# A hybrid decoder step on one core: the first weight loaded in two parts by rows, conditioning blocks moved ahead, the first block issued from GpSimd

## What is computed

```python
mod = (jax.nn.silu(c) @ w_ada + b_ada)[:, None, :]          # w_ada: 1024 x 6144 per layer
sh1, sc1, g1, sh2, sc2, g2 = jnp.split(mod, 6, axis=-1)
hn = rmsnorm(x, norm1_g) * (1.0 + sc1) + sh1
proj = hn @ w_in                                            # w_in: 1024 x 2560 per layer
xl, gl, bs, cs, hs = jnp.split(proj, 5, axis=-1)
# ... convolutions, a recurrence, an output projection and a residual,
# then a second norm, a convolutional FFN (1024 -> 2 x 2816 -> 1024), a residual;
# after two layers a last norm
```

## Time and profile before

| | us |
|---|---|
| median of three runs | 1335.13 |
| the three runs | 1335.13, 1333.09, 1335.45 |
| the profiled execution's own time | 1333.17 |
| its span, first to last instruction | 1331.5 |
| PE busy in the span | 1309.1 (98%) |
| DVE, ACT, POOL busy | 712.3, 488.1, 47.6 |
| mean granted TensorE clock | 0.997 of full speed |

### The profile page before, as it was taken

How to read it: one execution, slowest core, us unless ns; L and a number is a source line. 1 busy time by engine, 2 the same in 40 slices (tenths; PEclk the granted TensorE clock), 3 DMA queues, 4 the chain that set the end, 5 groups by cost and what they waited for, 6 DMA issues and landing times.

```text
span 1331.5 us, 23749 instructions
## 1 busy us (share of the span) xinstructions
PE 1309.1 (98%) x9767; PEld 1249.5 (94%) x9767; DVE 712.3 (53%) x1260; ACT 488.1 (37%) x646; POOL 47.6 (4%) x94
## 2 busy tenths in 40 slices
PE   7999999999999999999999999999999999999998
PEld 6887888899999999999999888999999999999997
DVE  5555854775445443454587177377544454354445
ACT  5424752453223222232353376245323322123231
POOL 0300000000000000000110000000000000000001
PEclk9999999999999999999999999999999999999999
DMA  9654656422221221212233465312222222222202
GB/s 307 213 184 161 218 196 216 159 95 71 88 95 63 95 96 63 95 63 95 80 128 117 168 222 186 131 64 72 72 97 93 80 95 68 90 80 78 95 32 97
DMA packets 115837, 157.10 MB, mean 118 GB/s; under 512 B 3543, under 2 KB 108984, under 8 KB 110645
## 3 DMA queue, kind: packets, MB, share of 16 engines
q1 hardware_dynamic: 108413, 112.55, 25.7%
q0 software_dynamic: 7168, 43.47, 9.5%
q10 hardware_dynamic: 184, 0.06, 0.0%
HBM read 153.08 MB, written 2.99 MB: 117 GB/s over the span
## 4 chain that ended last, share of the span: by engine, by line
PE 90%; DVE 3%; DMA 3%; SPq 2%; ACT 1%; issue 1%; DVEq 0%; POOLq 0%; ACTq 0%
PE ps L385 25%; PE ps L387 24%; PE ps L386 24%; PE ps L404 4%; PE ps L406 3%; PE ps L405 3%; PE ps L451 3%; DMA ada_w<-in_w_ada 2%; DVE w_lo L1051 1%; DMA ada_first<-in_w_ada 1%; SPq L280 1%; PE ps L651 1%; SPq L271 1%; SPq L253 1%; ACT w_hi L746 0%
## 5 line engine op out<-in xcount | busy, mean ns | idle before, releaser
L385 PE MATMUL ps<-norm_hi,w_hi 128*128 128x288 f32 x1792 | 533.1, 297 | 0.0
L386 PE MATMUL ps<-norm_lo,w_hi 128*128 128x288 f32 x1792 | 528.6, 295 | 0.0
L387 PE MATMUL ps<-norm_hi,w_lo 128*128 128x288 f32 x1792 | 526.8, 294 | 0.0
L385 PEld LDWEIGHTS ps<-norm_hi,w_hi 128*128 128x128 f32 x1792 | 335.8, 187 | 16.8 <-issue 15.9
L387 PEld LDWEIGHTS ps<-norm_hi,w_lo 128*128 128x128 f32 x1792 | 337.4, 188 | 0.0
L386 PEld LDWEIGHTS ps<-norm_lo,w_hi 128*128 128x128 f32 x1792 | 336.4, 188 | 0.0
L1051 DVE TENSOR_TENSOR w_lo<-w_raw,w_hi 128x2048 fp32r<-128x2048 f32 x91 | 208.4, 2290 | 86.6 <-ACT w_hi L746 86.5
L746 ACT ACTIVATE w_hi<-w_raw 128x2048 fp32r<-128x2048 f32 x91 | 173.9, 1911 | 156.3 <-PE ps L387 152.0
L385 PE MATMUL ps<-mid_hi,w_hi 128*128 128x288 f32 x704 | 209.3, 297 | 0.0
L386 PE MATMUL ps<-mid_lo,w_hi 128*128 128x288 f32 x704 | 207.7, 295 | 0.0
L387 PE MATMUL ps<-mid_hi,w_lo 128*128 128x288 f32 x704 | 207.0, 294 | 0.0
(11 more groups left out here) (213 smaller groups left out, 1381.0 us busy)
## 6 DMA issues: line engine op xcount, KB each, us to landing
w_raw<-in_ffn_w_up SPq DMA_DIRECT2D x44, 1024.0 KB, 5.0
ada_w<-in_w_ada POOLq DMA_DIRECT2D x40, 1024.0 KB, 5.1
w_raw<-in_w_in SPq DMA_DIRECT2D x20, 1024.0 KB, 5.1
w_raw<-in_ffn_w_down SPq DMA_DIRECT2D x16, 1024.0 KB, 5.2
ada_first<-in_w_ada SPq DMA_DIRECT2D x8, 1024.0 KB, 10.4
w_raw<-in_w_out SPq DMA_DIRECT2D x8, 1024.0 KB, 5.4
w_raw<-in_ffn_w_down SPq DMA_DIRECT2D x8, 768.0 KB, 4.4
work<-in_x_prompt SPq DMA_DIRECT2D x4, 512.0 KB, 5.3
```

The source lines that it names most:

```text
L385: T.matmul(out, WH[:, r, k, c:c + P], xh[:, k, h, :], start=start, stop=False)
L386: T.matmul(out, WH[:, r, k, c:c + P], xl[:, k, h, :], start=False, stop=False)
L387: last = T.matmul(out, WL[:, r, k, c:c + P], xh[:, k, h, :], start=False, stop=stop)
```

## The change

Five things are changed, all in the first 60 us:

1. **Two parts by rows.** The first two pieces of `w_in` are no longer loaded whole. A load brings the row blocks 0 to 3 of a piece (512 KB, semaphore `raw_rows`), a later one the row blocks 4 to 7 (512 KB, `raw_full`). ACT's `head_split` waits for the part that it reads.
2. **Order of SP's queue.** Now: c, x, first rows of both pieces, block 1, block 2, later rows of both pieces, block 3, vectors and states. Block 2 still waits for product 0, block 3 for product 1.
3. **Block 0 from GpSimd.** Its two loads are issued by GpSimd, after its small constants and ahead of the zeroing of `gate_w`.
4. **Sigmoid table.** ACT's table for the sigmoid is loaded as its first instruction, ahead of the nine vector loads.
5. **The later rows' split moves.** ACT splits the later rows after `first_row(2)` instead of before `first_row(1)`, DVE's two `head_low` for them stand in the rounds 4 and 5, and PE waits for the slot that a tile needs (`lo_done` 3 for tiles 0 and 1, 4 for tile 2).

The core of the diff:

```diff
-            first_block(0)
-            for s in range(2):
-                load(s, s, a["w_in"][0:1, :, 256 * s:256 * s + 256])
+            def load_rows(part, s):
+
+                src = a["w_in"][0, :, 256 * s:256 * s + 256].rearrange("(k p) c -> p k c", p=P)
+                k = slice(0, KX // 2) if part == 0 else slice(KX // 2, KX)
+                sp.dma_start(RAW[:, s, k, :], src[:, k, :]).then_inc(raw_full[s] if part else raw_rows[s], 16)
+
+            load_rows(0, 0)
+            load_rows(0, 1)
             first_block(1)
+            first_block(2)
+            load_rows(1, 0)
+            load_rows(1, 1)
+            first_block(3)
             vectors(sp, 0, slice(NFIRST, None), v_in[0])
-            first_block(2)
-            first_block(3)
...
             nc.gpsimd.memset(EPST[:], EPS).then_inc(ident_ready, 1)
+            ada0 = a["w_ada"][0].rearrange("(k p) c -> p k c", p=P)
+            for j in range(2):
+                pool.dma_start(FIRST[0][:, :, j, :], ada0[:, :, j * D:j * D + 256]).then_inc(first_full[0], 16)
             nc.gpsimd.memset(BLK[:], 0.0).then_inc(pool_step, 1)
...
-                if k == KX // 2:
-                    pe.wait_ge(lo_done, 4)
                 for h in range(2):
                     if k % 2 == 0:
                         pe.wait_ge(norm_ready, k + h + 1)
                     for i in range(3):
+                        if k == KX // 2 and h == 0 and i != 1:
+                            pe.wait_ge(lo_done, 3 + i // 2)
...
             act.sem_inc(ada_rows_ready, 1)
+            act.preload_act_table(ACT.Sigmoid)
             vectors(act, 0, slice(0, NFIRST), v_first)
...
-                if part == 0:
-                    act.wait_ge(raw_full[s], 16)
+                act.wait_ge((raw_full if part else raw_rows)[s], 16)
...
-            head_split(0, 1)
-            head_split(1, 1)
             for b in range(1, 4):
                 first_row(b)
+                if b == 2:
+                    head_split(0, 1)
+                    head_split(1, 1)
...
-            head_low(0, 1)
-            head_low(1, 1)
             for b in range(1, 4):
                 first_modulation(b)
                 sample_part(1, MOD_SH1, 2 * b)
+                if b == 2:
+                    head_low(0, 1)
                 scaled(1, 2 * b + 1, rs0)
                 sample_part(1, MOD_SH1, 2 * b + 1)
                 norm_low(1, 2 * b)
+                if b == 2:
+                    head_low(1, 1)
```

More of the change, by code:

```diff
@@ L199, in hybrid_trunk_kernel @@
         raw_full = [sem("raw_full0"), sem("raw_full1")]
+        raw_rows = [sem("raw_rows0"), sem("raw_rows1")]
         hi_done, lo_done = sem("hi_done"), sem("lo_done")
```

## The result

The changed kernel is slower: 1338.51 us median of 8 runs (1337.17 to 1340.09), against 1334.62 (1333.09 to 1336.64) of 8 runs of the kernel before, ratio 1.0026 with a 95% interval of 1.0017 to 1.0035. The forecast was 1333.5 with a range of 1330.2 to 1336.9: wrong in sign, and outside its range.

What follows compares the result with a forecast made beforehand. Bound by transferred bytes until 38 us, then TensorE; product 3's start was followed: 46.04 - (43.1 + 2.2) = 0.7 us gained, taken from the runs' mean: 1334.2 - 0.7 = 1333.5, range 1330.2 to 1336.9.

Steps and rivals of the forecast that it cites:

- Bytes in front of the blocks: Loads ahead of conditioning blocks: block 1 3.0 us earlier, block 2 3.9, block 3 at 42.9, capping the gain at 3.1.
- TensorE's side: TensorE from product 0 to product 3 without DMA waits: start of product 3 at 43.1, gain 2.9 us.
- Moved splits, vectors at the end, SyncE's waits: Later rows' splits, late vectors and SyncE's waits before blocks 2 and 3: each costed at nothing.
- the third rival: SyncE's waits empty the DMA queue, blocks 2 and 3 land late: gain 0 or slightly below, counted with the forecast.
- Block 0 from GpSimd: Block 0's loads compete with x tiles at the start: product 0 ends 2.2 us later, bounds 0.5 and 3.3.
- x's landing: Last x tiles fall behind GpSimd's loads of block 0: x5 lands at 15.2, bounds 11.5 to 16.9.
- The end of both streams: x tiles and block 0 together: bytes as before, the last lands at 17.4 - 0.5 = 16.9.
- What follows x: Serial chain from x5's square, begun about 15.7, to product 0; a faster clock could give back 1.6 us.
- The page that spoke against the change: Skill page on queues taking turns by packet: x and block 0 end near 16.4, change worth -0.1 us; set aside.
- That block 0 hides behind x: Rival: GpSimd's loads reach the engines after the x tiles; gain 2.9 us (2.4 to 3.8), 1331.3; chance 0.35.
- The slow clock in the filler: Rival: 16 filler products after product 0 at 1.2 GHz, 3.4 us late, 1336.9; chance 0.15 with other large product 0 delays.
- the end shows what product 3 shows: Nothing behind product 3 has its own time: what its start (46.04 before) gains, the kernel gains.

Runs made afterwards that it cites:

- experiment 1: The changed kernel with block 0 issued by SyncE again, behind the x tiles, the other four edits kept: 1331.24 us, ratio 0.998.
- experiment 6: The changed kernel with block 0 back on SyncE and a few more filler products on TensorE: 1331.45 us, ratio 0.9974.
- experiment 7: The changed kernel with block 0 back on SyncE and layer 0's vectors between the loads of blocks 1 and 2: 1332.08 us, ratio 0.9986.
- experiment 9: The changed kernel with block 0 back on SyncE and no early sigmoid table: 1331.34 us, ratio 0.9973.
- experiment 3: The changed kernel with GpSimd waiting for the landing of x4 before it issues block 0: 1337.72 us, one run.
- experiment 4: The changed kernel with block 0 issued from ScalarE's queue, behind its nine small loads: 1337.38 us, one run.
- experiment 5: The changed kernel with filler products ahead of the transposes of x1, x2 and x3: 1339.41 us, ratio 1.0046; repeated, 1337.00, ratio 1.0021.
- the second run of 9: The kernel of experiment 6 (block 0 on SyncE, more fillers) without the early sigmoid table: 1331.19 us, ratio 0.9976.
- experiments 2: The kernel before with one edit alone, block 0 issued from GpSimd: 1338.21 us, ratio 1.0036.
- experiment 8: The changed kernel with GpSimd's block 0 held until x4 lands and SyncE's later loads held until block 0 lands: 1333.12 us, one run.

## Why the prediction was wrong, point by point

**Bytes in front of the blocks: right, the close match in part luck.** Worked out: 2.9 us if product 0 ended where it did, and 1331.3 for that case. Measured in experiment 1: 2.85 in the medians, and 1331.24. But product 0 ended 0.86 us later there than in the trace of before, and the gain at product 3 was 2.19; most of the rest of the 2.85 comes from the kernel before, whose median lies 0.9 above its profiled execution. The wall at block 3's landing was 43.4 without GpSimd's head start; measured 43.5 to 43.7 (experiments 1 and 6). The vectors: 0.9 worked out, 1.0 at block 3's landing (experiment 7).

**TensorE's side: right.** The sum was product 0's end + 8.53 + 5.41 + 7.70 + 1.0. For the changed kernel that is 28.75 + 22.64 = 51.39, measured 51.26; for experiment 1 it is 21.35 + 22.64 = 43.99, measured 43.85, and for experiment 7 22.28 + 22.64 = 44.92, measured 44.77. So the statement that each microsecond of product 0's delay is a microsecond of product 3's held over 8 us.

**Moved splits, vectors at the end, SyncE's waits: right at nothing.** There is no wait in front of products 1, 2 and 3. SyncE did stand for 23 us in its blocks' issues, to 29.8, and the DMA engines ran dry (29 GB/s at 26 us), which was the third rival's mechanism, but no product waited for it.

**The sigmoid table: right at nothing** (experiment 9).

**Block 0 from GpSimd: this step failed.** It took product 0's end to be 2.2 us late, with bounds of 0.5 and 3.3; measured 8.26 against the trace of before, and 7.40 against experiment 1, which lacks this edit alone. The term is the only one that was far off, and its error is the whole of the miss: 43.1 + 2.2 = 45.3 was forecast for product 3, 51.26 came. It failed in three places:
- *x's landing.* Taken: x5 at 15.2, bounds 11.5 to 16.9. Measured: x3 at 18.2, x5 at 18.7. I read the earlier trace rows as two streams that meet, of which the earlier goes first. They are hardly that. In the trace of before the queues from 135.0 to 135.5, three microseconds after SyncE issued its load, show GpSimd's alone:

```profile
q0 software_dynamic: 28, 0.23, 108.2%
```

SyncE's packets are seen only from 135.5 on, when GpSimd's load was nearly in. Why they came so late there was not tried; but the row can't tell how two running streams divide the engines, and experiments 3 and 4 can. Turns a packet at a time, with packets of 4 KB on both sides, give half and half, and then the last of x lands as late as block 0.
- *The end of both streams.* Taken from the earlier trace rows as 16.9, for the bytes were as before. Measured 18.7. While the two ran together the engines moved 339 GB/s between 9 and 10 us, where x alone had moved 414. (The 299 between 17 and 18 are SyncE's packets already, 287 of them against one of GpSimd's.) Part of this is no effect of sharing: in experiment 1 too x5 landed 1.2 and block 0 1.0 us later than in the trace of before.
- *What follows x.* I took the chain from x5's square onward as it had been, and the square 0.5 us after the landing. It was 3.3 behind: the copy of the first spreading stands ahead of it, and that comes out of transposes that now begin only when x3 lands. TensorE, without work from 7.5 to 11.3 and again around 17, was at PEclk 0.50 (1.2 GHz) from about 10.5 until 27. From x3's landing to product 0's end: 9.5 us before, 10.55 after, 7.96 with fillers and the clock at full speed (experiment 5). So 8.26 is 7.2 (x3's landing) less 1.5 (the chain behind it, which before had queued squares and a product 0 at the lower clock) plus 2.6 (the clock), within the rounding; the three parts are read from single traces. The prediction named the clock, but as something that could give back 1.6 us; it took 2.6 instead.

**The page that spoke against the change.** What the Trainium skill says in DMA: Bandwidth & Descriptors, section "Queues, rings and completion order" (turns between queues, a packet at a time), agrees with the 92 packets to 88, 130 to 134, 84 to 84 and 337 to 336 above; I set it aside for a row that did not show two running streams. By that rule I had worked out x and block 0 together at 16.4 and -0.1 us. That too was far too mild: the rule had the order right, but I had carried on from it with the engines' full rate and TensorE's chain as before.

**The rivals.** That block 0 hides behind x: false, GpSimd's packets moved from 5 us on, and the issue took 0.98 us for 1024 runs, near the 1.1 of the slope. Its price, 1331.3, is that of the kernel without that edit. The slow clock in the filler: not in the changed kernel's trace (L544 took 3.82), but its mechanism, late x tiles and a TensorE at half speed, was at work one stage earlier, in the transposes, the spreading and product 0, and belonged into the forecast and not beside it. The range ended at 1336.9 because I added that rival's 3.4 us to a delay of 2.2 whose upper bound I had set at 3.3 from one misread row. By "the end shows what product 3 shows" the claim held: product 3 is 5.2 late and the profiled execution 5.7 longer; the medians differ by only 3.9, since the profiled execution of before was 1.45 below its median. Against experiment 1, 7.41 at product 3 stands beside 7.27 in the medians.

**The fastest version** is the changed kernel with block 0 back on SyncE, 1331.2 to 1331.5 with or without fillers and early table (ratios 0.9973 to 0.998): 0.2 to 0.3% faster than before and 0.5% faster than the changed kernel. With fillers, block 3's landing holds it (waits of 0.32 and 0.17 us in front of product 3 in experiment 6 and the second run of 9), so more would need fewer bytes in front of that block, or larger runs, which moved at 414 GB/s for x against 350; neither was tried.

## What to carry to other kernels

A second queue adds no bandwidth, it changes who gets it: the engines give each queue a packet in turn (84 and 84, for 0.23 and 0.09 MB), so an urgent load that stands first in its own queue is still slowed by whatever a second queue has running (experiments 2, 3 and 4). Moved to another queue, block 0 landed on time and left x in peace only where nothing else wanted the engines, and there it was the later loads, held back for it, that paid (experiment 8, 1333.12 in one run against 1331.24). Before a trace row is used against a rule, see that it shows the rule's case, here the packets by queue over a stretch in which both move data, and not two issue times and two landings. When a transfer slips at the start of a kernel, count the clock too: TensorE, idle for late tiles, did the work behind them at half speed, 2.6 of the 8.3 us in the trace, and about 1.3 us at the end of the kernel by the estimate of experiment 5.

## What the runs showed of the hardware that was not expected

- GpSimd's queue moved block 0 in packets of about 4 KB (92 packets for 0.38 MB), while SyncE's and ScalarE's moved the same block in packets of 1 KB (1732 for 1.74 MB in experiment 1, 336 for 0.34 MB in experiment 4), the length of its runs. The Trainium skill says in DMA: Bandwidth & Descriptors, section "SWDGE vs HWDGE vs iDMA", that a packet of the software path holds up to 4096 bytes preferably; the 4 KB here agree. It is no limit: GpSimd's load of the earlier trace rows, whose runs are 8 KB, shows 28 packets for 0.23 MB, 8 KB each.
- The larger packets were not faster: alone, GpSimd's block 0 moved at 328 GB/s from 12.5 to 18 us (experiment 8), SyncE's with 1 KB packets at 348 from 13 to 18 (experiment 1).
- A queue that joins another can move its first packet late: 5 us after GpSimd's issue in experiment 3 (9.28, first packets behind 14.4), 3 us in the changed kernel (2.02, none before 5.0), over 3 us for SyncE's load of the earlier trace rows, but under 2 us in experiment 8 (9.33, first packets between 11.0 and 11.3), where x was nearly in. What sets this was not tried.
- One load of 1024 runs cost GpSimd 0.98 us to issue; loads of 96 to 128 runs 0.55.
- A table load runs beside ScalarE's own DMA issues: with the early table it stands at 0.94 us in ScalarE's timeline, for 1.28 us, and the first small load was issued at 0.97.
